# Offsets on the priorities of task kinds in the list that orders a decoder layer's projection stage

## The reference

```
h = RMSNorm(x)
q, k, v, u, g_a, g_p = split(h @ w_in)        # widths 512, 512, 512, 512, 1024, 1024
q, k = rope(RMSNorm_per_head(q)), rope(RMSNorm_per_head(k))   # rope on 16 of 64 dims
A = block-sparse causal attention(q, k, v)    # 8 heads, blocks of 256 tokens, own block + best 3 past ones
B = (trailing means over 2/4/8/16 tokens of u, minus u) @ w_grp * scale
x = x + (sigmoid(g_a) * (A @ w_up_attn) + sigmoid(g_p) * (B @ w_up_pool)) @ w_out
x = x + relu(RMSNorm(x) @ w_ff1)^2 @ w_ff2
```

## Time and profile before

| | us |
|---|---|
| median of 3 runs | 937.29 (936.63 to 937.66) |
| the profiled execution, its own time | 936.56 |
| span of its slowest core (core 4) | 935.5 |
| spans of the 8 cores | 930.1 to 935.5 |
| PE busy in the span | 899.7 (96%) |
| DVE, ACT, POOL busy | 462.3, 364.8, 111.8 |

### The profile page before, as it was taken

One profiled execution on the slowest core, in us unless ns is written; L12 is line 12 of the kernel. 1 busy time (PEld: TensorE's weight loads), 2 busy tenths in 40 slices (PEclk: granted clock), 3 DMA queues, 4 the chain that ended last, 5 costly groups with the idle time before them and its releaser, 6 DMA issues.

```text
span 935.5 us, 17328 instructions; the slowest of 8 cores (930.1 to 935.5 us)
## 1 busy us (share of the span) xinstructions
PE 899.7 (96%) x5724; PEld 461.8 (49%) x5724; DVE 462.3 (49%) x870; ACT 364.8 (39%) x722; POOL 111.8 (12%) x197
## 2 busy tenths in 40 slices
PE   2899998999999999999999999999999999999998
PEld 1444454667777654444444444444444444444444
DVE  2788877647332233345774444444443444444443
ACT  3777455788999952221006223131101222111120
POOL 4212212221000000100201111001110111000000
PEclk9999999999999999999999999999999999999999
DMA  7963353244533363993996433023330333202113
GB/s 186 226 160 80 64 136 46 53 63 75 70 69 66 61 102 98 203 197 83 159 142 99 56 48 55 12 32 48 56 46 1 46 47 56 34 1 82 54 68 157
DMA packets 66342, 78.13 MB, mean 84 GB/s; under 512 B 35984, under 2 KB 54672, under 8 KB 66000
## 3 DMA queue, kind: packets, MB, share of 16 engines
q0 software_dynamic: 25056, 40.28, 28.9%
q1 hardware_dynamic: 41200, 36.75, 16.5%
HBM read 98.41 MB, written 8.39 MB: 114 GB/s over the span
## 4 chain that ended last, share of the span: by engine, by line
PE 88%; DMA 6%; DVE 2%; issue 1%; ACT 1%; SPq 0%; POOL 0%; DVEq 0%; ACTq 0%; POOLq 0%
PE bank L1370 24%; PE bank L1341 24%; PE bank L1013 11%; PE bank L433 8%; PE bank L1241 6%; PE bank L907 6%; PE bank L945 3%; DMA raw<-w_qkvu 3%; PE bank L1027 3%; PE bank L1032 3%; DMA raw<-x 2%; DMA raw<-w_slice 1%; PE bank L487 1%; PE bank L520 0%; DVE raw L377 0%
## 5 line engine op out<-in xcount | busy, mean ns | idle before, releaser
L1370 PE MATMUL bank<-raw 128*128 128x512 bf16 (+1 forms) x1032 | 223.2, 377 | 0.0
L1341 PE MATMUL bank<-raw 128*128 128x512 bf16 x1024 | 223.1, 379 | 0.0
L1348 ACT ACTIVATE raw<-bank 128x512 f32<-128x512 f32 x128 | 76.4, 597 | 375.6 <-PE bank L1341 317.0
L1370 PEld LDWEIGHTS bank<-raw 128*128 128x128 bf16 x1032 | 101.1, 98 | 120.2
L1341 PEld LDWEIGHTS bank<-raw 128*128 128x128 bf16 x1024 | 100.1, 98 | 120.9
L1350 DVE SCALAR_TENSOR_TENSOR raw<-bank,raw 128x512 bf16<-128x512 f32 x128 | 88.5, 692 | 140.0 <-ACT raw L1348 140.0
L914 ACT ACTIVATE raw<-bank 128x512 bf16<-128x512 f32 (+1 forms) x288 | 145.0, 580 | 24.6 <-PE bank L945 20.6
L1378 DVE SCALAR_TENSOR_TENSOR raw<-bank,raw 128x512 f32<-128x512 f32 x129 | 96.3, 746 | 113.5 <-PE bank L1370 112.8
L433 PE MATMUL bank<-raw 128*128 128x512 bf16 x512 | 121.2, 386 | 10.9 <-ACT raw L372 3.8
L1013 PE MATMUL bank<-raw 128*128 128x512 bf16 x512 | 123.0, 380 | 2.1 <-DMA raw<-w_slice 1.9
L907 PE MATMUL bank<-raw 128*128 128x256 bf16 x576 | 98.7, 268 | 0.8 <-ACT raw L914 0.3
(11 more groups left out here) (90 smaller groups left out, 578.2 us busy)
## 6 DMA issues: line engine op xcount, KB each, us to landing
raw<-x SPq DMA_DIRECT2D x32, 512.0 KB, 7.0
raw<-w_ff POOLq DMA_DIRECT2D x64, 256.0 KB, 4.0
raw<-w_slice POOLq DMA_DIRECT2D x22, 640.0 KB, 7.9
out<-raw SPq DMA_DIRECT2D x15, 512.0 KB, 2.7
raw<-w_qkvu POOLq DMA_DIRECT2D x8, 512.0 KB, 13.2
raw<-raw SPq DMA_DIRECT2D x2, 1024.0 KB, 4.5
raw<-w_out POOLq DMA_DIRECT2D x4, 512.0 KB, 13.1
raw<-c_ind POOLq DMA_DIRECT2D x4, 256.0 KB, 5.2
```

The lines of the kernel that those rows point to most:

```text
L1341: t.group("pe", [lambda e, c=c, j=j, bk=bk: e.matmul(bank_f(bk), lhsT=ffw1[s][:, c, j * 128:(j + 1) * 128], rhs=hT[:, c, tg * 512:(tg + 1) ...
L1348: t.op("act", lambda e, bk=bk, si_=si_: e.activation(out=sqz[si_], in_=bank_f(bk), func=AF.Square), reads=hb[bk], writes=[b_sqz[si_]])
L1370: t.group("pe", [lambda e, j=j, bk=bk, i=i, c0_=c0_, c1_=c1_, n_=n_: e.matmul(bank_f(bk)[:, 0:n_], lhsT=a1T[ab][:, j, i * 128:(i + 1) * 12 ...
```

## The change

A table of offsets is added to the priorities of 19 kinds of tasks before the list is made, and the window of candidates shrinks from 0.12 to 0.09 us. Nothing else changes: the same tasks, the same assumed durations, the same loads. Of the table's numbers the positive ones (later) are those of qev, xsq, xld, kev, pj_q, pj_k, trd, mul and ev, the negative ones (earlier) those of rope, pj_v, pj_u, sq, bev, band, vev, red, root and uev.

```
+        PRIO = {"qev": 5, "rope": -5, ..., "pj_v": -4, "band": -2,
+                ..., "vev": -1.5}
+        for k_ in tasks:
+            k_.prio += PRIO.get(k_.name, 0.0)
...
-            cand = [b_ for b_ in best if b_[0] <= t0_ + 0.12]
+            cand = [b_ for b_ in best if b_[0] <= t0_ + 0.09]
```

More of the change, by code:

```diff
@@ L766, in build_nc @@
         add("xdone", 0.0, [("pool", 1.0, x_done)], deps=[hev[tt] for tt in range(NT)])
+        PRIO = {"qev": 5, "rope": -5, "red": -1, "xld": 3.5, "kev": 3, "uev": -0.5, "xsq": 4, "sq": -2.5,
+                "mul": 0.5, "bev": -2.5, "pj_u": -2.5, "ev": 0.5, "trd": 1, "pj_v": -4, "band": -2,
+                "pj_q": 1.5, "root": -1, "pj_k": 1, "vev": -1.5}
+        for k_ in tasks:
+            k_.prio += PRIO.get(k_.name, 0.0)
         LAT = 0.2
```

## The result

The changed kernel takes 949.55 us (947.3 to 950.07), the kernel before 937.34 in the same runs: a ratio of 1.0127, 95% interval 1.0109 to 1.0144, so 12.2 us slower. The prediction was 938.7 with a range that ended at 942.6. Some executions show the cores of one die at a lower granted clock and take some per cent longer; they are left out of every ratio here, which leaves two executions for the late slice load, three for the changed kernel again and 4 to 12 for each of the others.

The account below looks back on a forecast made before the run. PE, busy 96% of the span, was taken as the bound. +1.4 us before attention and +0.7 - 0.4 at its start made +1.7, taken as +1.5: 936.56 became 938.1, as a median 938.7; range 934.3 to 942.6.

Parts of the forecast that it names:

- four new waits: 34.5 to 60 us: the changed order gives PE four new waits, 5.0 us in sum against 1.90 before.
- (a): 34.5 to 60 us: PE waits 0.8 us for transposed tile 4, evicted behind the scale of k's job 3.
- (b): 34.5 to 60 us: PE waits 0.7 us for the mul of tile 5, now behind a scale, eviction and rope.
- (c): 34.5 to 60 us: tiles 7 and 8 squared ahead of evictions; PE waits 0.45 for a mul, 0.95 for a rope.
- (d): Near 57 to 59 us: tile 10's square precedes k job 5's root; PE waits 2.1 us for that job's rope.
- I take the same arrivals: Loads of x: tiles land when they did before, tile 9 at 50.51 us, tile 10 between 54.5 and 54.76.
- +10.4: Attention's start: the first gate piece follows about 10.4 us after the first scores.
- even: Attention's start: 9.7 us from first scores to first gate piece would be no loss; 0.7 more forecast, 0.4 taken off.
- the rival of a costlier start: Attention's start: later or repeated clock falls, a slow rope and a late hand-off give 942 us; chance 0.25, including more waits.
- the slow rope: Attention's start: the moved rope's third step on POOL takes 1.28 us instead of 0.32, adding 0.9 us.
- The hidden waits: 34.5 to 60 us: tiles 7 to 10 land in time, 3.5 us of waits vanish, 935.2 us; chance 0.2.
- the nothing case: Whole kernel: PE is the bound, waits shift about and the sum stays, 937.3 us; chance 0.1.

Follow-up runs that it names:

- the late slice load: The changed kernel with only the second weight slice's load issued by POOL at attention step 16 instead of step 10; 1.0057 of the kernel before.
- the changed kernel again: The changed kernel measured once more, unaltered, on the chip of the later runs; 1.0114 of the kernel before.

## Why the prediction was wrong

- **The four new waits were right in kind, and their sum on core 4 nearly in size.** Estimated 5.0 us of idle time from 34.5 to 60, measured 4.06 on core 4 and 4.95 on core 2. One by one: (a) 0.25 and (b) 0.32 for 0.8 and 0.7, (c) 1.06 for 0.45 + 0.95, (d) 2.04 for 2.1, of which 0.84 lies behind 60. The 1.11 at 57.13 for a transposed tile was not foreseen.
- **"I take the same arrivals" failed.** The reason given was SP's unchanged order and a load always under way. But each load waits for a mul that frees its slot, and the prediction itself had the mul of tile 5 end at 43.05: the load of tile 9 left at 43.67, and the tile was squared at 53.36 instead of 50.51. That wait (d) still came out right on core 4 is luck: PE too came to it 1.5 us later (58.80 instead of 57.3). On other cores it was up to 3.5 us.
- **60 to 90 was mis-sized on the slow core.** 0.85 predicted, 1.26 on core 4 (0.84 of it the end of (d)), 3.86 on core 2 (1.65 the end of (d), 2.04 a wait at 88.18 for a scale, 0.4 in the prediction), where the clock was 0.92.
- **The first scores came at 159.0 on core 4 for 158.1, a mean of 160.1 over the cores.** That is 5.7 us of moved work and 3.5 of waits and clock, where the prediction had 1.4.
- **Attention's start cost more than "+10.4".** 12.1 us on core 4; in the mean 12.5 against 9.7 for even (15.4 less 5.7): +2.8, not +0.7 - 0.4. The moved rope took 1.84 us (162.43 to 164.27 on core 4), the short case of the earlier trace rows. Half-speed time was in it, as the rival of a costlier start had it: a granted clock of 0.86 in that stretch on core 4, 0.62 on core 2, 0.78 in the mean against 0.93 in the kernel before, with 4.3 us of PE's idle time against 3.3. With two jobs put back there the clock was 0.99 (above). The Trainium skill (GPSIMD Engine Reference, Specifications) has POOL share its SBUF interfaces with VectorE; the slow rope that was priced by that did not come. "Beside a busy DVE" was too wide a condition, and the trace of the kernel before could have told: its slow third step at 98.30 runs beside the main instruction of a mul, which reads two tensors of SBUF, and no mul is left when attention starts.

```profile
98.12 1.28 DVE L399 SCALAR_TENSOR_TENSOR raw<-raw 128x1024 bf16<-128x1024 f32 x1 [0.17 <-DVE raw L397]
```

- **The largest term was put at nothing without a reason: "Behind 190 us nothing moves", and no cost from the first gate piece to there.** Behind the first gate piece the mean is 770.6 us against 766.7, and the late slice load gives all of it back (766.2). On core 4 it lies from 171 to 190. What was missing: a load that hangs on the end of the list moved beside SP's transposes, and PE waited 5.1 us in the mean for what they held up.
- So, in means over the cores: +3.5 ahead of the first scores, +2.8 to the first gate piece, +3.9 behind; 10.2 us. The time goes by the slowest core, which is 13.0 us longer (948.5 for 935.5) at a mean clock of 0.987. It took more than one term to leave the range: with the load late alone the ratio is 1.0057, which at 937.34 is 942.7, still just above 942.6.
- The last step of the sum holds a slip: 938.1 and 0.7 make 938.8, not 938.7.
- **The rivals.** The costlier start ended at 942, and had the right sign and place of one part. The hidden waits and the nothing case fell: without the collision the change is still at 1.0057.

## What to carry to other kernels

When a reordering empties a list sooner, look up everything that hangs on "list empty" (fences, loads) and what each queue then meets; carry the sum on to the first point where both kernels' queues stand alike. A scheduler that counts a load too short makes every priority table a gamble: measure the pace of arrival, put it into the model, and then try tables; here the same table went from 1.0057 to 0.9983, while the measured pace without the table gave 1.0013. A load's start is set by the task that frees its slot, so follow each moved task to the buffer that it frees.

## What the runs showed of the hardware

- Two DMA transposes (1088 packets, 0.26 MB) landed in 2.4 us each ahead of a load of 640 KB, and in 8.2 us each beside it (medians of core 4; 6.1 to 8.6 over the cores). The cost hangs on what waits for them: PE waited 5.1 us where DVE came to the overwrite 3.6 us behind their start, and 2.1 where it came 6.4 behind it (means of the cores).
- The clock behind a PE wait is not told by the length of that wait: 3.56 us kept 1.00, 2.4 us lost it, in one execution. The Trainium skill (TensorE: Matmul & The Clock Gate, What's actually happening) has it follow how busy PE was; these rows neither bear that out nor speak against it.
- POOL's third rope step (L477) has two lengths in all runs and cores: 1.13 to 1.29 us in the 360 cases in which a mul's L399 runs on DVE meanwhile, 0.32 to 0.33 in the 936 in which none does, whatever else DVE runs.
- The 8 cores run the same rows in the same order and yet ended at 939.9 to 948.5 us in one execution: (d) was 2.0 to 3.5 us by core, and half-speed time followed it on some.
